# Expert gate/up weights loaded as eight consecutive rows per partition, token rows gathered without a permuted copy

## The reference, cut to what matters

```
h = layer_norm(DN_ALPHA * h + mix, ln1_g, ln1_b)
scores = sigmoid(h @ router_w)                 # 8 of 64 experts per token, weights gw
for each expert e, for its tokens tok:
    gate, up = split(h[tok] @ w_gu[e])         # w_gu[e]: 1024 x 512
    y = (silu(gate) * up) @ w_down[e]          # w_down[e]: 256 x 1024
    acc[tok] += y * gw[tok, e]
h = layer_norm(DN_ALPHA * h + acc + shared(h) + ple, ln2_g, ln2_b)
```

## Time and profile before

| | |
|---|---|
| median of 3 runs | 2564.52 us (2564.05 to 2569.41) |
| the profiled execution, its own time | 2562.0 us |
| its span in the trace | 2560.0 us |
| PE busy | 2439.3 us, 95% of the span |
| DVE, ACT, POOL busy | 900.5, 423.2, 793.3 us |
| moved by DMA | 391.36 MB |
| gate/up loads, issue to landing | 24.6 us median, 64 of 2 MB |
| indirect gathers of rows, issue to landing | 6.2 us median, 306 |
| adds to the scratch rows, issue to landing | 9.2 us median |

### The profile page before, as it was taken

The page is one execution under the profiler, slowest core; times in us unless marked ns, Lnnn a source line. Parts: engine busy times, 40 slices in busy tenths (PEclk is TensorE's granted clock), DMA queues, the critical chain, the costliest instruction groups (busy, mean ns, idle before and its releaser), DMA issues. The chain is left out here.

```text
span 2560.0 us, 26577 instructions
## 1 busy us (share of the span) xinstructions
PE 2439.3 (95%) x10446; PEld 1480.8 (58%) x10446; DVE 900.5 (35%) x1540; ACT 423.2 (17%) x665; POOL 793.3 (31%) x764
## 2 busy tenths in 40 slices
PE   6999999999999999999999999979999999999991
PEld 3444554345799544444445544457777777776761
DVE  5011553675533532323323262222222223323325
ACT  1001122335454110010001110001111111111110
POOL 3000111101343100000001135326666666676642
PEclk9999999999999999999999999989999999999996
DMA  6201003100000211111050501079999999999995
GB/s 250 90 33 45 22 33 104 41 17 9 1 1 26 91 49 49 32 43 49 25 206 25 188 30 50 26 291 349 343 343 345 347 345 349 342 345 347 348 321 165
DMA packets 167964, 391.36 MB, mean 153 GB/s; under 512 B 19706, under 2 KB 40234, under 8 KB 167072
## 3 DMA queue, kind: packets, MB, share of 16 engines
q1 hardware_dynamic: 135248, 300.64, 32.2%
q0 software_dynamic: 31584, 82.00, 12.3%
q10 hardware_dynamic: 1008, 7.02, 0.7%
HBM read 322.50 MB, written 67.11 MB: 152 GB/s over the span
## 5 line engine op out<-in xcount | busy, mean ns | idle before, releaser
L1856 PEld LDWEIGHTS banks<-arena 128*128 128x128 f32 x4096 | 523.8, 192 | 75.8 <-DMA arena<-in_exp_w_gu 39.4
L1856 PE MATMUL banks<-arena 128*128 128x128 f32 (+7 forms) x4096 | 533.8, 292 | 30.8 <-DMA arena<-in_exp_w_gu 28.4
L2276 POOL DMA_INDIRECT arena<-hp_scratch,arena x306 | 294.8, 964 | 243.6 <-issue 80.2
L1380 PE MATMUL banks<-arena 128*128 128x512 f32 x672 | 291.8, 594 | 1.3 <-PEq L736 1.3
L328 PE MATMUL banks<-arena 128*128 128x512 f32 x640 | 280.9, 596 | 4.6 <-DVE arena L1093 4.3
L1864 PE MATMUL banks<-arena 128*128 128x512 f32 (+1 forms) x528 | 237.4, 592 | 1.4 <-DVE arena L2240 0.9
L1380 PEld LDWEIGHTS banks<-arena 128*128 128x128 f32 x672 | 127.8, 190 | 163.1 <-issue 163.1
L328 PEld LDWEIGHTS banks<-arena 128*128 128x128 f32 x640 | 120.0, 190 | 159.4 <-issue 149.7
L280 POOL TENSOR_SCALAR arena<-arena 128x1 f32<-128x1 f32 x16 | 15.5, 970 | 604.6 <-DVE arena L271 604.6
L2291 POOL DMA_INDIRECT acc_scratch<-arena x99 | 153.7, 1552 | 66.8 <-DMA acc_scratch<-arena 42.1
L321 PE MATMUL banks<-arena 128*128 128x512 f32 x384 | 168.4, 597 | 0.6 <-PE banks L321 0.6
(11 more groups left out here) (364 smaller groups left out, 2517.4 us busy)
## 6 DMA issues: line engine op xcount, KB each, us to landing
arena<-in_exp_w_gu SPq DMA_DIRECT2D x64, 2048.0 KB, 24.6
arena<-in_exp_w_down SPq DMA_DIRECT2D x64, 1024.0 KB, 20.2
arena<-in_w_in SPq DMA_DIRECT2D x10, 2048.0 KB, 9.3
arena<-in_w_in SPq DMA_DIRECT2D x12, 1024.0 KB, 6.2
arena<-in_w_branch SPq DMA_DIRECT2D x12, 512.0 KB, 7.2
hp_scratch<-arena SPq DMA_DIRECT2D x10, 512.0 KB, 2.9
arena<-hp_scratch,arena POOLq DMA_INDIRECT x306, 6.3
arena<-in_x SPq DMA_DIRECT2D x4, 1024.0 KB, 14.8
```

Of the source, the lines that this page charges most:

```text
L1380: last = nc.tensor.matmul(PS[:, g % 4, :], lhs[:, k, :], rhs[:, k, :], start=(k == 0), stop=(k == 3))
L1856: last = nc.tensor.matmul(PS[:, bank + part, f * n:(f + 1) * n], weights[:, k, part * FF + f * P:part * FF + (f + 1) * P], x[:, k, 0:n], s ...
L2276: nc.gpsimd.indirect_dma_start(out=rows[0:n, :], out_offset=None, in_=table, in_offset=bass.IndirectOffsetOnAxis(ap=at, axis=0)).then_inc( ...
```

## The change

The view of the gate/up matrices becomes "e (p k) n -> e p k n": partition p holds the eight consecutive rows 8p to 8p+7, which are 16 KB in one piece. For the channels to match, DVE's transposes read the gathered quarters with columns in the order (j, c), a step of 8 floats between neighbours, where before they read 32 neighbouring floats at a time. The gathers take their quarters from the plain rows in `hx_d`, and the permuted copy goes: the eight ACT copies, the eight stores, two stores of zero rows at the start, their buffers and semaphores. The eight TensorE transposes of a spilled block read their columns with the same step of 8. The down matrices, the shared expert and the number and size of the gathers stay.

```diff
-        hp_d = nc.dram_tensor("hp_scratch", (SEQ + PADR, D), F32).ap()
...
-                    sp.dma_start(hp_d[pads, :], zero).then_inc(pads_in, 16)
...
-                act.wait_ge(pads_in, 144)
+                act.wait_ge(pads_in, 112)
...
-        gu_v = a["exp_w_gu"].rearrange("e (k p) n -> e p k n", p=P)
-        hq_d = hp_d.rearrange("s (q c) -> (s q) c", q=4)
+        gu_v = a["exp_w_gu"].rearrange("e (p k) n -> e p k n", p=P)
+        hq_d = hx_d.rearrange("s (q c) -> (s q) c", q=4)
...
-                def permuted_out(t):
-                    sp.wait_ge(o_perm, t + 1)
-                    sp.dma_start(hp_d[t * P:(t + 1) * P, :], hp[t % 2]).then_inc(o_sp[t % 2], 16)
-
-                for t in range(NT - 2):
-                    permuted_out(t)
...
-                        last = nc.tensor.transpose(PS[:, k // 4, (k % 4) * P:(k % 4 + 1) * P], xg_spill[:, k * P:(k + 1) * P], ident)
+                        last = nc.tensor.transpose(PS[:, k // 4, (k % 4) * P:(k % 4 + 1) * P], xg_spill[:, k:D:KD], ident)
...
-                    if j:
-                        act.wait_ge(o_n, t + 1)
-                        if t >= 2:
-                            act.wait_ge(o_sp[t % 2], 16 * (t // 2))
-                        nc.scalar.activation(hp[t % 2].rearrange("p (q c j) -> p q c j", q=4, c=QC),
-                                             h[:, t, :].rearrange("p (c q j) -> p q c j", q=4, c=QC), ACT.Copy).then_inc(o_perm, 1)
...
-                    src = rows[r % 2][:, 0:n * QD].rearrange("p (g c j) -> p g c j", g=n, j=32)
+                    src = rows[r % 2][:, 0:n * QD].rearrange("p (g j c) -> p g c j", g=n, j=32)
...
-                for i in range(2):
-                    pool.wait_ge(o_sp[i], 8 * NT)
```

More of the change, by code:

```diff
@@ L1528, in build @@
         up = [carve(HALF, R2 + i * HALF) for i in range(2)]
-        hp = [carve(D, CONSTS["level"][0] + i * D) for i in range(2)]
-        assert CONSTS["level"][0] + 2 * D <= CONSTS["ranks"][0]
         wg = carve(KD * D, base).rearrange("p (j k n) -> p j k n", j=2, k=KD)
@@ L1575, in build @@
                                     "capacity", "cols", "rows", "tables", "pos"))
-        o_perm, o_sp = sem("o_perm"), [sem(f"o_store_perm{i}") for i in range(2)]
         e_slots = [sem(f"e_slots{i}") for i in range(2)]
@@ L1659, in _ @@
                     sp.dma_start(wg[:, j, :, :], wg_v[:, :, j * HALF:(j + 1) * HALF]).then_inc(f_wg, 16)
-                permuted_out(NT - 2)
-                permuted_out(NT - 1)
                 sp.wait_ge(o_n, NT)
@@ L2263, in _ @@
                     nc.gpsimd.tensor_tensor(hs, hs, up[q % 2], ALU.mult).then_inc(f_hid, 1)
-                pool.wait_ge(pads_in, 144)
+                pool.wait_ge(pads_in, 112)
                 pool.wait_ge(e_pos, 1)
```

## The result

Over 22 runs each, the changed kernel takes 2572.62 us in the median and the kernel before 2563.86 us. The ratio is 1.003 with a 95% interval of 1.0024 to 1.0036: a loss of 6 to 9 us, small, but the interval lies clear of 1. One run of each kernel took far longer (3279.85 us before, 4215.84 us after, the latter at a granted clock of 0.578 in place of 0.98) and is left out of the ratio. The profiled execution has a span of 2567.7 us, 7.7 us more than before.

A forecast was written before the change was run, and what follows sets the result against it. TensorE was taken to bound the early loop, DMA the last 176 us; with adds at 12.5 us per place, 2562.0 + 12.1 - 0.8 - 0.9 = 2572.4 us, predicted as 2575 us since the profiled execution lies 2.5 below the median; range 2546 to 2606.

The forecast's parts named there:

- What bounds the kernel: Expert loop: TensorE sets the pace in the first 600 us, the DMA engines in the last 176 us.
- The gain of longer rows: Gate/up loads on q1: 0.93 us less per place, ending TensorE's waits in the last stretch, -14.0 to -14.9 us.
- The adds are later: q0's adds wait behind q1's 16 KB packets: 2.4 us more per add, between 0 and 7.0 us.
- queues take turns row by row: DMA engines alternate queues one packet each, whatever its size; q0 waits 0.617 us per packet of its own.
- The path: Each place's adds wait for those before: the add chain goes from 10.1 to 12.5 us per place.
- The stretches: Expert loop at 12.5 us per place: second stretch nothing, third +12.1 us, last -0.8 us.
- The first wait: First gate/up load, 22.43 us from issue to landing, gets 0.9 us shorter.
- The transposes: DVE's step of 8: 0 to +0.8 us each, hidden by 2.4 us of cover; as rival about 2590 us, chance 0.03.
- The spilled block's weight loads: TensorE's eight weight loads with the step: +1.1 us at double time, at best 0; taken as 0.
- The removed copies: Eight ACT copies of 1.075 us have no waiter, so their end gives 0; -8.6 us if ACT were the bound.
- A number that I had named as the judge: Adds' time to landing, 9.2 us before: near 11.6 the main case is right, near 10 the first rival.
- All of the gain: Rival: adds and gathers late by less than 1.4 us, TensorE never waits; 2548.7 us, chance 0.34.

The follow-up runs named there:

- g1: The changed kernel with adds of odd places sent to a second accumulator, so an add waits for the one two places before: 2567.77 us, 1.0009 to the kernel before.
- f3: The kernel before with only the transposes changed, to read with a step of 8 columns: 2564.27 us, 1.0 to the kernel before.
- f2: The kernel before with 16 KB gate/up rows and the permuted copy kept, so transposes read consecutive columns: 2571.28 us, 1.0027 to the kernel before.
- g4: The changed kernel with each gate/up load split in eight, packets of 2 KB as before: 2563.83 us, 0.9999 to the kernel before.
- g2: Control for g1: the kernel before (2 KB rows) with adds of odd places sent to a second accumulator: 2569.78 us, 1.0022 to the kernel before.
- e3: The kernel before without the permuted copy, with plain rows and 2 KB weight rows, on another chip: 2675.37 us, 0.9977 to the kernel before.

## Why the prediction was right, and where its path and its sizes were off

The forecast of 2575 us met 2572.62 us, with the right sign and the right cause, q0's transfers delayed by q1's longer rows. That it came so close is partly luck: the path to TensorE was incomplete, and errors in the stretches cancel. Step by step:

- **What bounds the kernel.** Right: with 4 KB rows the last stretch falls to TensorE's pace, and the second and third don't move.
- **The gain of longer rows** was mis-sized for the loop. I took 0.93 us per place from two loads that ran alone. In the loop, 1850 to 2232 us, the queue of the changed kernel reads

```profile
q1 hardware_dynamic: 12319, 93.72, 62.9%
q0 software_dynamic: 13675, 37.68, 37.8%
```

  That is 0.629 x 382 x 16 / 93.72 = 41.0 us of an engine per MB, against 0.655 x 6112 / 92.66 = 43.2. A place loads 3.15 MB over 16 engines: 8.07 against 8.50 us, 0.43 us less. That is 5%, where the two rows alone gave 16% for gate/up. It was still enough to end TensorE's waits for weights. With 4 KB rows most of it is there already, 0.641 x 6112 / 94.23 = 41.6 us per MB:

```profile
q1 hardware_dynamic: 25400, 94.23, 64.1%
```

- **The adds are later.** Right in kind and near in size: 2.4 us were foretold, and an add takes 11.9 where it took 10.0 us, and 11.5 (issued at 2234.40) where it took 9.4. That the length of the rows does it is shown by the table above. That queues take turns row by row is not: equal counts would also come of turns of several rows each. I read more out of them than they hold, and no run tests the turn itself.
- **The path** was incomplete. The step "the add chain then takes 12.5 us per place" made the wait of an add for its neighbour the only bound and had no term for rows that reach TensorE late. From 1700 to 2275 us POOL waited 23 times for its own adds; the add at 2234.40 did not wait for the one at 2222.00, though they lie 12.4 us apart. g1 took that wait away, and its profile has 225.8 us in the third stretch. What reached TensorE were rows that came late, at 7 of 40 places. How much of that is the neighbour's wait, the two y buffers or the gathers' own delay stays open. The clock that fell behind two of the gaps wasn't in the sum.
- **The stretches.** Foretold 0, +12.1 and -0.8 us; measured +4.5, +9.5 and -5.9. I set a mean place against a mean add, which gives nothing for a stretch whose mean place is longer. But waits come at single places: two gaps of 1.95 and 0.6 us and one group of matmuls at the lower clock, 1.65 us longer, make 4.2 of the 4.5 us of the second stretch. The last stretch was counted at 12.5 us per place and took 170.03 / 14 = 12.1. The errors cancel in part: +10.4 foretold in all, +7.7 in the spans.
- **The first wait.** Its chain row went from 22.43 to 19.49 us, 2.9 us less instead of 0.9. I have no cause for the other 2 us:

```profile
1680.93 19.49 DMA arena<-in_exp_w_gu
```

- **The transposes.** Right: 2025 against 1245 ns for 1024 columns is 0.76 ns per column, the 0.78 of the two small adds. f3 shows that the cover hides it with 2 KB rows. At the places where TensorE waits for rows the cover is gone, and the trace alone would charge the step up to 0.8 us each; f2, without the step, is no faster (1.0027 against 1.0023), so what it adds to the loss is too small to tell. The Trainium skill ("SBUF — State Buffer", section "Door 1: The DMA port swizzle") has a cost for each new line of 16 bytes. The trace agrees that a step of 32 bytes costs time, 0.76 ns per column. ACT pays more for the same step, 1.0 us for 1024 columns.
- **The spilled block's weight loads** take 0.188 us with the step against 0.142, 0.4 us for eight; I had bounded them at 1.1.

```profile
L1912 PEld LDWEIGHTS banks<-arena x8: 186/188/190, 2500.5 to 2501.6; 128*128 128x128 f32 x8
```

- **The removed copies** gave nothing that can be told, as said (g4, together with the step and the eight loads).
- **A number that I had named as the judge failed.** The adds' median to landing reads 6.1 us after and 9.2 before. Runs with the same loop (f3 6.2, g2 9.2) differ as much, so that median says nothing; issue to release in the timeline does.
- **The rivals.** "All of the gain" wanted 2548.7 us, 15.8 below; 4 KB rows come to 10.4 below their own kernel before. The gain was there, and the length of the rows took it. On the rule of the Trainium skill about turns of many descriptors ("DMA: Bandwidth & Descriptors", section "Queues, rings and completion order") no run of this set decides, since its turns would grow with the row as well.
- **The range** went from 2546 to 2606 us, while its two ends were worked out as 2548.7 and 2608; both lack the 2.5 us between the profiled execution and the median. It was wide enough for gain and loss alike, so that the time fell in it says little.

## What to carry to other kernels

Longer DMA rows were cheaper per byte here (43.2 to 41.0 us of an engine per MB), but with them the transfers of another queue came about 2 us later. Where a queue with short, urgent packets runs beside the stream, choose the shortest row that takes most of the gain (here 4 KB, 0.9964, not 16 KB, 1.0023); splitting the load by rows is a change of two lines. And before a wait is called the bound, look for other paths through the same late transfers, and judge a run that takes the wait away by its own control: set against the changed kernel of another set, g1 wins back over half of the loss, and against its own control all of it.

## What the runs showed of the hardware that was not expected

On different chips the same kernel took 2564 and 2681 us. Loops with 2 KB rows moved 344 GB/s on the one and 310 (e3) on the other, and 16 KB rows with contiguous transposes gave 1.0027 and 0.9918. The verdict on a change to the transfers can turn with the chip. ACT reading with a step of 8 floats took 2.08 us instead of 1.075 for 1024 columns, 1.0 us more, where DVE's transpose takes 0.8 us more.
